# ScalarE scales the first nine token tiles, with two joint reciprocals; VectorE builds a second state table earlier

## The chip, the cores and the metric

The kernel runs on one core of a Trainium2 chip. The metric is the device time of one execution, in microseconds (us). The engines are TensorE (PE in the profile), VectorE (DVE), ScalarE (ACT), GpSimd (POOL) and SyncE (SP, which here only issues DMAs). Each engine works through its own instruction stream in order; streams wait for one another through semaphores.

## The reference, cut to what matters

One layer of a hybrid diffusion backbone in float32, for 1024 latent tokens and 128 context tokens of width 1024:

```python
def _layer(x, cvec, p, rows, h0):
    sh1, sc1, g1, sh2, sc2, g2 = _adaln(cvec, p["w_ada"], p["b_ada"])   # silu(c) @ w_ada + b_ada, six parts
    h = _rmsnorm(x, p["norm_mix"]) * (1 + sc1) + sh1                    # x * rsqrt(mean(x*x) + eps) * g
    proj = jnp.dot(h, p["w_in"])
    pool_out = _pool_mixer(proj[..., :D_POOL], p["pool_w"], p["pool_scale"], rows)
    ssm_out, finals = _ssm_mixer(proj[..., D_POOL:], p, h0)             # diagonal state space, both directions
    mix = jnp.dot(jnp.concatenate([pool_out, ssm_out], axis=-1), p["w_out"])
    x = x + g1 * mix
    h = _rmsnorm(x, p["norm_mlp"]) * (1 + sc2) + sh2
    f = jnp.square(jax.nn.relu(jnp.dot(h, p["w_mlp1"])))
    return x + g2 * jnp.dot(f, p["w_mlp2"]), finals
```

The change touches the first `_rmsnorm`, the division of each token by its root mean square, and the point in time at which one of the weight tables for `_ssm_mixer` (powers of the diagonal times the input matrix) is computed.

## The kernel before, in words

The tokens are nine tiles of 128 tokens by 1024 channels, `XS[0]` to `XS[8]`, the last one the context. The order of all work is written out by hand: one block of code for each engine, with semaphores between them. The opening, up to the input projection, goes as follows.

- **TensorE** forms two parts of the conditioning rows, shift and scale: 16 weight tiles of w_ada (`ada_unit`, L1344, two matmuls with two output rows each and 512 columns), as they land by DMA, and the bias rows (L1361). Then the four half rows that ScalarE copies out of PSUM (`ROW0`, L589) are turned into columns (L1367), one after the other: there is one `ROW0` buffer, so ScalarE copies half row k only when half row k-1 is turned (`ada_cols`), and TensorE turns it when it is copied (`row_ready`). After the fourth, `turn_tile` (L1377) transposes the token tiles one by one; it waits for the scaled tile (`xn`), before tile 1 also for the finished conditioning columns (`ada0`), and from tile 2 on for `affine` to have freed the PSUM banks of the tile two before. Beside tiles 4 to 8 run parts of the first two blocks of the input projection (`project`, L1331 to L1333: three passes with the high and low halves of both operands).
- **ScalarE** computes for each tile, as it lands, the sum of squares (`stats`, L538) and the root (L540, semaphore `root`), then the four half rows, then half of each `affine` (L549), the rounding of the result into its high half (L555) and the high halves of the weights (L576).
- **VectorE** computes the tables of the discretised state matrix, its powers, the table `power_chain` (L1017 to L1028) and one 128x1024 state table, `to_state(1, 1, 0, 0)` (L926, L927, L930). It then scales the nine tiles (`normed`: a reciprocal of one column, L949, and a multiply by it, L950), waits for the four turned half rows (`ada_cols`), makes the conditioning columns out of them (L974, L1041, semaphore `ada0`), and goes on to its half of `affine` (L959) and to the low halves (L964, L969). After the ninth low half seven more state tables follow, with two or three low halves of weights between them; the last of the seven is `to_state(1, 1, 1, 7)`, in front of `split_lo(4)`, and then comes the scan over the states (L1061 to L1069), whose stages wait for ScalarE's copies of the states (`st_act`).
- **TensorE** turns the state tables (`turn_wb`, L1421) between blocks of the input projection, four matrices at a time, as VectorE's tables (`wbt`, for the first one `wbt_first`) come.

Of the later stages only their order matters here: input projection and first scan, kernels of the state space and second scan, output projection, a second normalisation (where ScalarE already scales the tiles by a column, L826), and from about 420 us on the MLP.

Of the kernel before, what the change touches and what calls it, by code (L numbers as in the profile page):

```python
# [19 lines left out]
ALU = mybir.AluOpType  # L20
ACT = mybir.ActivationFunctionType
# [6 lines left out]
TT = T // P  # L28
TG = 384
NG = T // TG  # L30
L = 8
# [31 lines left out]
def build(nc, x_prompt, x_sample, state_ssm, c, c_ctx, norm_mix, norm_mlp, w_ada, b_ada, w_in, w_out, pool_w,  # L63
          pool_scale, ssm_a_re, ssm_a_im, ssm_log_dt, ssm_b_re, ssm_b_im, ssm_c_re, ssm_c_im, ssm_d,
          ssm_w_glu, w_mlp1, w_mlp2, norm_out, inv_count, y_prompt, y_sample, new_state):
    V, S, PE, GP = nc.vector, nc.scalar, nc.tensor, nc.gpsimd
# [57 lines left out]
    STAT = [STATS[:, i, :] for i in range(3)]  # L124
# [60 lines left out]
    def scratch(name, shape):  # L185
# [10 lines left out]
             "wbt", "wbt_first", "wbt_mm", "wb_ready", "st_mm", "st_part", "st_act", "st_dve", "cs_in", "c_mm", "c_ready", "dd_in", "dd_ready",  # L196
             "pad_zero", "rz_zero", "pad_act", "pad_read", "inv_in", "inv_read", "pooled", "pw_in", "map_mm", "map_ev",
             "ca_ready", "kk_mm", "kk_ready", "loc_in0", "loc_in1", "filled", "cx_h", "y_mm", "y_ev", "yd_w0", "yd_w1", "yd_g", "yr0", "yr1", "yr2",
             "row2", "cols2", "gates_w", "acts", "part_ev", "gated", "xt_in0", "xt_in1", "xc_in", "root_inv", "gb_in", "y_split_hi", "y_split", "so", "so_hi",
             "mix_hi", "mix_pool", "mix_ready", "acc", "f_ready", "fin_mm", "fin_ready", "fin_out", "no_in",  # L200
             "y_final", "out_w", "tabs", "ada0", "sqr"]
    sem = {n: nc.alloc_semaphore(n) for n in names}
    s = type("Sems", (), sem)
# [311 lines left out]
    def _(act):  # L515
# [21 lines left out]
        def stats(t, src, dump, base):  # L537
            S.activation(dump, src, ACT.Square, accum_out=STAT[0][:, t:t + 1]).then_inc(s.sq, 1)  # L538
            act.wait_ge(s.sq, base + t + 1)
            S.activation(STAT[1][:, t:t + 1], STAT[0][:, t:t + 1], ACT.Sqrt, bias=EPSB[:], scale=1.0 / D).then_inc(s.root, 1)  # L540
# [35 lines left out]
            S.activation(w_split_bufs(w)[0][:], RAW[n % 4][:], ACT.Copy).then_inc(s.w_hi, 1)  # L576

        act.wait_ge(s.tabs, 2)
        for t in range(TT):
            act.wait_ge(x_in[t], 16 if t < L else 16 * L)  # L580
            stats(t, XS[t][:], SQ0[:], 0)

        n_row = 0
        for part in range(2):
# [68 lines left out]
        for a in range(NG * N_IN):  # L653
            i, g = IN_SEQ[a]
            project(a)
            for k in WB_AT.get(a, ()):
                turned_wb(k)
            if g == NG - 1 and i + 2 < N_IN:
                split_hi(i + 2, FIRST_IN + i + 2)
            if a in (7, 8):  # L660
                for p_ in range(8 * (a - 7), 8 * (a - 6)):
                    if p_ == 12:
                        act.wait_ge(s.wbt, 7)
                    states_out(p_)
            for b in C_AT.get(a, ()):
                c_out(b)
# [200 lines left out]
    def _(dve):  # L867
        count = [0]

        def then(ins):  # L870

            count[0] += 1
            ins.then_inc(s.dve, 1)
            dve.wait_ge(s.dve, count[0])
# [43 lines left out]
        def to_state(b, d, h, ready):  # L918
            gs = slice(b * GB + 8 * h, b * GB + 8 * h + 8)
            q0 = d * G + gs.start  # L920
            out = WB[b][:, d, 8 * h:8 * h + 8, :].rearrange("n g (j p) -> n g j p", p=SP)
            powers = [t_[:, L - 1::-1, q0:q0 + 8] if d == 0 else t_[:, 0:L, q0:q0 + 8] for t_ in (PR, PI)]
            pr, pi = (t_.rearrange("n e q -> n q e").unsqueeze(3).to_broadcast([P, 8, L, SP]) for t_ in powers)
            b1, b2 = (t_[:, q0:q0 + 8, :].unsqueeze(2).to_broadcast([P, 8, L, SP]) for t_ in (B1, BY))
            tmp = TPQ[:, 0:8 * P].rearrange("n (g j p) -> n g j p", g=8, p=SP)
            tt(tmp, b2, pi, ALU.mult).then_inc(s.dve, 1)  # L926
            tt(out, b1, pr, ALU.mult).then_inc(s.dve, 1)  # L927
            count[0] += 2
            dve.wait_ge(s.dve, count[0])
            tt(out, out, tmp, ALU.add).then_inc(s.wbt if ready else s.wbt_first, 1)  # L930
            dve.wait_ge(s.wbt if ready else s.wbt_first, max(ready, 1))

        def from_state(b, d, h):
            q0 = d * G + b * GB + 8 * h
# [8 lines left out]
            dve.wait_ge(s.dve, count[0])  # L943
            tt(out, out, tmp, ALU.add).then_inc(s.ca_ready, 1)
            dve.wait_ge(s.ca_ready, 4 * b + 2 * d + h + 1)

        def normed(t, src, dst, base):
            dve.wait_ge(s.root, base + t + 1)
            then(V.reciprocal(STAT[2][:, t:t + 1], STAT[1][:, t:t + 1]))  # L949
            ts(dst, src, STAT[2][:, t:t + 1], None, ALU.mult).then_inc(s.xn, 1)  # L950

        def affine(t, ht, ada, base):
            cond = 0 if t < L else 1
# [62 lines left out]
        def power_chain():  # L1016
# [3 lines left out]
            for i in range(6):  # L1020
# [7 lines left out]
                then(ts(di, di, 2.0, None, ALU.mult))  # L1028
                sr, si = AR_[i][:], AI_[i][:]

        power_chain()
        to_state(1, 1, 0, 0)
        for t in range(TT):
            normed(t, XS[t][:], XS[t][:], 0)
        dve.wait_ge(s.ada_cols, 4)
        for k in range(4):
            cols = BANK[7][:, 64 + 8 * k:72 + 8 * k].rearrange("p (k a) -> p a k", a=2)
# [152 lines left out]
        to_state(1, 0, 0, 5)  # L1190
        split_lo(3, FIRST_IN + 3)
        to_state(1, 0, 1, 6)
        to_state(1, 1, 1, 7)
        split_lo(4, FIRST_IN + 4)
        def beside_first(k):
            if k in SPLIT_AT:
# [128 lines left out]
    def _(pe):  # L1325
# [80 lines left out]

        def turn_wb(k):
            b, d, i = k // 8, k // 4 % 2, k % 4
            if k in (12, 13):
                pe.wait_ge(s.wbt_first, 1)  # L1410
            else:
                pe.wait_ge(s.wbt, min(k // 2 + 1, 7))
            if k == 0:
                pe.wait_ge(s.aff_a, 4 * TT)
                pe.wait_ge(s.aff_d, 4 * TT)
            if 4 <= k < 8 or k >= 12:
                pe.wait_ge(s.wb_ready, k - 3)
            elif k >= 8:
                pe.wait_ge(s.st_act, k + 5)
            for q in range(4):  # L1420
                last = PE.transpose(BANK[4 + k % 4][:, q * P:(q + 1) * P], WB[b][:, d, 4 * i + q, :], ID[:])  # L1421
            last.then_inc(s.wbt_mm, 1)
# [278 lines left out]
```

## Time and profile before

| | us |
|---|---|
| median of 3 runs (lowest, highest) | 1302.23 (1300.67, 1304.34) |
| the profiled execution | 1306.17 |
| its span, first to last instruction | 1304.1 |

| engine | busy us | share of the span |
|---|---|---|
| TensorE, matmul | 1219.2 | 93% |
| VectorE | 857.9 | 66% |
| GpSimd | 473.4 | 36% |
| ScalarE | 329.1 | 25% |

The mean granted clock of TensorE is 0.968 of full speed. The busy share is an average over stages: TensorE is busy nearly throughout from about 82 us on, with gaps up to 315 us, and mostly waits before that. What a change in the opening is worth has to be read from the engines' instructions in order of time, and from what each of them waited for.

### The profile page before, as it was taken

The page shows a single profiled execution, that of the slowest core. Times are in us where ns is not written, and L with a number is a line of the kernel's source. Part 1 is how long each engine was busy: PE and PEld are TensorE (multiplying, and loading weights), DVE is VectorE, ACT ScalarE, POOL GpSimd, SP SyncE. Part 2 cuts the span into 40 slices and gives each one's busy share as a digit, 9 for nine tenths or more (in the row PEclk, how much of TensorE's full clock was granted, in tenths as well). Part 3 has the DMA queues.
Part 4 walks back from the last instruction along what each step waited for, and adds up shares of the span by engine and source line. Part 5 has one row for each costly group of instructions (what it writes and reads, how often), then busy time and mean ns, then how long its engine had stood idle before and what let it go on. Part 6 is the DMA issues. An engine that isn't in the chain of part 4 may idle for free.

```text
span 1304.1 us, 18626 instructions
## 1 busy us (share of the span) xinstructions
PE 1219.2 (93%) x6479; PEld 1057.5 (81%) x6479; DVE 857.9 (66%) x1343; ACT 329.1 (25%) x613; POOL 473.4 (36%) x394
## 2 busy tenths in 40 slices
PE   3779989895899999999999999999999999999994
PEld 0179978564697888899899899899899899899893
DVE  2988798999886487564564564664664664654658
ACT  2374333222523476011011011011011011021023
POOL 1100000220100341743733733734724724625626
PEclk9979999887899999999999999999999999999997
DMA  8913423875611332120120120110110110210004
GB/s 182 320 34 105 111 74 102 242 175 144 203 42 61 91 104 81 33 65 25 39 64 16 48 64 16 48 58 22 48 49 18 62 48 16 64 48 16 32 0 145
DMA packets 79369, 101.63 MB, mean 78 GB/s; under 512 B 25762, under 2 KB 61766, under 8 KB 79076
## 3 DMA queue, kind: packets, MB, share of 16 engines
q1 hardware_dynamic: 56848, 80.00, 20.2%
q0 software_dynamic: 5200, 17.67, 4.6%
q10 hardware_dynamic: 17284, 3.47, 1.4%
q8 instruction: 23, 0.38, 0.1%
q14 instruction: 14, 0.11, 0.0%
HBM read 89.53 MB, written 9.49 MB: 76 GB/s over the span
## 4 chain that ended last, share of the span: by engine, by line
PE 80%; DVE 8%; issue 3%; DMA 3%; POOL 2%; ACT 2%; ACTq 1%; SPq 0%; POOLq 0%; DVEq 0%
PE bank L1331 23%; PE bank L1332 23%; PE bank L1333 23%; DMA raw<-in_w_ada 2%; POOL acc L511 2%; PE bank L1344 2%; PE bank L1524 1%; PE bank L1523 1%; PE bank L1463 1%; ACTq L525 1%; PE bank L1377 1%; PE bank L1522 1%; DVE x_lo L964 1%; DVE fold_p L1063 1%; DVE fold_q L1061 1%
## 5 line engine op out<-in xcount | busy, mean ns | idle before, releaser
L511 POOL TENSOR_TENSOR acc<-acc,gated 128x512 f32<-128x512 f32 x288 | 401.4, 1394 | 400.7 <-DVE gated L1295 361.6
L1331 PE MATMUL bank<-x_hi,w_hi 128*128 128x384 f32 x960 | 325.2, 339 | 4.2 <-issue 2.7
L1332 PE MATMUL bank<-x_lo,w_hi 128*128 128x384 f32 x960 | 322.4, 336 | 0.0
L1333 PE MATMUL bank<-x_hi,w_lo 128*128 128x384 f32 x960 | 322.3, 336 | 0.0
L1295 DVE TENSOR_TENSOR gated<-bank,gate_b 128x512 f32<-128x512 f32 x288 | 194.1, 687 | 115.9 <-PE bank L1333 87.5
L1331 PE MATMUL bank<-w_hi,f_hi 128*128 128x512 f32 x576 | 224.4, 390 | 1.8 <-DVE w_lo L1276 1.2
L1333 PE MATMUL bank<-w_hi,f_lo 128*128 128x512 f32 x576 | 224.4, 390 | 0.0
L1332 PE MATMUL bank<-w_lo,f_hi 128*128 128x512 f32 x576 | 224.4, 390 | 0.0
L850 ACT ACTIVATE relu<-bank 128x384 f32<-128x384 f32 x96 | 47.2, 492 | 649.5 <-PE bank L1333 646.5
L1285 DVE TENSOR_TENSOR f_tmp<-relu 128x384 f32<-128x384 f32 x96 | 66.4, 691 | 211.6 <-ACT relu L850 211.6
L1331 PEld LDWEIGHTS bank<-x_hi,w_hi 128*128 128x128 f32 x960 | 181.4, 189 | 8.3 <-issue 6.6
L1332 PEld LDWEIGHTS bank<-x_lo,w_hi 128*128 128x128 f32 x960 | 181.5, 189 | 0.6
L1333 PEld LDWEIGHTS bank<-x_hi,w_lo 128*128 128x128 f32 x960 | 181.4, 189 | 0.0
L1331 PEld LDWEIGHTS bank<-w_hi,f_hi 128*128 128x128 f32 x576 | 108.1, 188 | 25.0 <-DVE w_lo L1276 1.5
L1333 PEld LDWEIGHTS bank<-w_hi,f_lo 128*128 128x128 f32 x576 | 108.1, 188 | 22.6
L1332 PEld LDWEIGHTS bank<-w_lo,f_hi 128*128 128x128 f32 x576 | 108.1, 188 | 22.1
L1276 DVE TENSOR_TENSOR w_lo<-raw,w_hi 128x1024 fp32r<-128x1024 f32 x62 | 96.4, 1554 | 0.0
L841 ACT ACTIVATE w_hi<-raw 128x1024 fp32r<-128x1024 f32 x62 | 63.7, 1053 | 0.0
L1289 DVE TENSOR_TENSOR f_lo<-f_tmp,f_hi 128x384 fp32r<-128x384 f32 x96 | 53.6, 558 | 3.3
L1344 PE MATMUL bank<-raw,vector_cols 128*2 128x512 f32 x64 | 31.2, 632 | 22.0 <-ACT vector_cols L527 16.4
L499 POOL TENSOR_TENSOR acc<-acc,x_again 128x512 f32<-128x512 f32 x18 | 25.0, 1391 | 54.0 <-DVE acc L1181 54.0
L1344 PEld LDWEIGHTS bank<-raw,vector_cols 128*2 128x2 f32 x64 | 4.9, 88 | 46.6 <-issue 17.6
(301 smaller groups left out, 1422.1 us busy)
## 6 DMA issues: line engine op xcount, KB each, us to landing
raw<-in_w_mlp SPq DMA_DIRECT2D x64, 512.0 KB
raw<-in_w_ada SPq DMA_DIRECT2D x48, 512.0 KB
x_tile<-in_x_sample POOLq DMA_DIRECT2D x8, 512.0 KB, 8.5
raw<-in_w_in SPq DMA_DIRECT2D x8, 512.0 KB
raw<-in_w_out SPq DMA_DIRECT2D x8, 512.0 KB
x_again<-in_x_sample POOLq DMA_DIRECT2D x8, 512.0 KB, 3.8
out<-acc SPq DMA_DIRECT2D x8, 512.0 KB, 2.6
u_rows<-proj ACTq DMA_DIRECT2D x4, 576.0 KB, 3.1
```

What stands on the lines that cost most here:

```text
L499: GP.tensor_tensor(ACC[:, t, half], ACC[:, t, half], XT[t % 2][:, half], ALU.add).then_inc(s.acc, 1)
L511: GP.tensor_tensor(a, a, BT[i % 4][:], ALU.add).then_inc(s.acc, 1)
L841: S.activation(w_split_bufs(w)[0][:], RAW[n % 4][:], ACT.Copy).then_inc(s.w_hi, 1)
L850: S.activation(RL[i % 2][:], BANK[i % 4][:, 0:TG], ACT.Relu).then_inc(s.ev_act, 1)
L1276: tt(lo[:], RAW[n % 4][:], hi[:].bitcast(F32), ALU.subtract).then_inc(s.w_split, 1)
L1285: tt(FT[i % 2][:], RL[i % 2][:], RL[i % 2][:], ALU.mult).then_inc(s.sqr, 1)
L1289: tt(FL[:, m, cols], FT[i % 2][:], FH[:, m, cols].bitcast(F32), ALU.subtract).then_inc(s.f_ready, 1)
L1295: tt(BT[i % 4][:], BANK[(6 + i) % 4][:], GBT[:, cond, (i % 2) * 512:(i % 2) * 512 + 512], ALU.mult).then_inc(s.ev_dve, 1)
L1331: mm(out, sh_, mh, start=first, stop=False)
L1332: mm(out, sh_, ml, start=False, stop=False)
L1333: return mm(out, sl, mh, start=False, stop=last)
L1344: last = mm(BANK[banks[hf]][0:2, :], cv, RAW[n % 4][:, hf * 512:hf * 512 + 512], start=(k == 0), stop=False)
```

## The change

ScalarE scales the nine tiles by itself, after all nine roots and in front of the half rows, with the instruction `Copy` and a column as its scale. VectorE makes the reciprocals in two instructions, one for the first seven tiles ahead of `power_chain` and one for the last two behind it. The state table `to_state(1, 1, 1)` moves from behind `to_state(1, 0, 1)` to directly behind `to_state(1, 1, 0)`, ahead of the wait for `ada_cols`, and counts on another semaphore (`wbt_first`), so that the waits for `wbt` are counted anew.

```diff
         act.wait_ge(s.tabs, 2)
+        def normed(t):
+            act.wait_ge(s.root_inv0, 1 if t < L - 1 else 2)
+            S.activation(XS[t][:], XS[t][:], ACT.Copy, scale=STAT[2][:, t:t + 1]).then_inc(s.xn, 1)
+
         for t in range(TT):
             act.wait_ge(x_in[t], 16 if t < L else 16 * L)
             stats(t, XS[t][:], SQ0[:], 0)
+        for t in range(TT):
+            normed(t)
...
                     if p_ == 12:
-                        act.wait_ge(s.wbt, 7)
+                        act.wait_ge(s.wbt, 6)
...
-            tt(out, out, tmp, ALU.add).then_inc(s.wbt if ready else s.wbt_first, 1)
-            dve.wait_ge(s.wbt if ready else s.wbt_first, max(ready, 1))
+            tt(out, out, tmp, ALU.add).then_inc(s.wbt if ready > 0 else s.wbt_first, 1)
+            dve.wait_ge(s.wbt if ready > 0 else s.wbt_first, ready if ready > 0 else 1 - ready)
...
-        def normed(t, src, dst, base):
-            dve.wait_ge(s.root, base + t + 1)
-            then(V.reciprocal(STAT[2][:, t:t + 1], STAT[1][:, t:t + 1]))
-            ts(dst, src, STAT[2][:, t:t + 1], None, ALU.mult).then_inc(s.xn, 1)
...
+        dve.wait_ge(s.root, L - 1)
+        V.reciprocal(STAT[2][:, 0:L - 1], STAT[1][:, 0:L - 1]).then_inc(s.root_inv0, 1)
         power_chain()
+        dve.wait_ge(s.root, TT)
+        V.reciprocal(STAT[2][:, L - 1:TT], STAT[1][:, L - 1:TT]).then_inc(s.root_inv0, 1)
         to_state(1, 1, 0, 0)
-        for t in range(TT):
-            normed(t, XS[t][:], XS[t][:], 0)
+        to_state(1, 1, 1, -1)
         dve.wait_ge(s.ada_cols, 4)
...
         to_state(1, 0, 1, 6)
-        to_state(1, 1, 1, 7)
         split_lo(4, FIRST_IN + 4)
...
-            if k in (12, 13):
-                pe.wait_ge(s.wbt_first, 1)
+            if k >= 12:
+                pe.wait_ge(s.wbt_first, k // 2 - 5)
             else:
-                pe.wait_ge(s.wbt, min(k // 2 + 1, 7))
+                pe.wait_ge(s.wbt, k // 2 + 1)
```

## Rows read from the trace of the kernel before

**Rows 1.** Windows: busy us of each engine in a stretch, and the granted clock

```profile
core 0: us, PE busy (x) PEld busy (x) DVE busy (x) ACT busy (x) POOL busy (x), PEclk, DMA share, GB/s
...
62.00:66.30 4.30, 2.09 (x18) 1.77 (x18) 4.12 (x11) 1.76 (x3) 0.00 (x0) 0.70 0.48 143
66.30:74.50 8.20, 7.00 (x32) 6.03 (x32) 6.16 (x20) 4.72 (x10) 0.00 (x0) 0.54 0.00 1
...
82.00:87.00 5.00, 4.81 (x18) 4.75 (x19) 2.49 (x6) 0.65 (x1) 0.00 (x0) 0.50 0.15 45
```

**Rows 2.** Chain of waits, 0 to 330 us: start, duration, what

```profile
62.55 0.59 ACT ada_row L589
...
65.65 0.58 PE bank L1367 x4
66.24 1.90 PE bank L1377 x8
68.14 1.17 issue
69.31 1.95 PE bank L1377 x8
```

**Rows 3.** ScalarE in order of time: start, duration, line, out<-in [idle before]

```profile
54.84 0.57 ACT L589 ACTIVATE ada_row<-bank 2x512 f32<-2x512 f32 x1
...
65.01 0.59 ACT L589 ACTIVATE ada_row<-bank 2x512 f32<-2x512 f32 x1 [0.73 <-PE bank L1367]
69.24 1.50 ACT L549 ACTIVATE h_tile<-bank,ada_cols,ada_cols 128x128 f32<-128x128 f32 x4 [3.64 <-DVE ada_cols L1041]
71.29 1.50 ACT L549 ACTIVATE h_tile<-bank,ada_cols,ada_cols 128x128 f32<-128x128 f32 x4 [0.54 <-PE bank L1377]
```

**Rows 4.** VectorE in order of time, 56 to 70 us

```profile
56.79 1.22 DVE L926 TENSOR_TENSOR fold_pq<-b_im_re,pow_im 128x1024 f32<-128x1024 f32 x1
...
60.44 0.16 DVE L949 RECIPROCAL stats<-stats 128x1 f32<-128x1 f32 x1
...
68.19 0.74 DVE L974 SCALAR_TENSOR_TENSOR ada_cols<-bank,vector_cols 128x4 f32<-128x4 f32 x4
```

**Rows 5.** The nine scaling instructions by tile: shortest, median, longest ns, first and last start

```profile
L950 DVE TENSOR_SCALAR x_tile<-x_tile,stats x9: 752/753/754, 60.6 to 67.5; 128x1024 f32<-128x1024 f32 x9
```

**Rows 6.** ScalarE in order of time, in the second normalisation

```profile
470.75 1.16 ACT L826 ACTIVATE xn_tile<-acc,stats 128x1024 f32<-128x1024 f32 x1 [1.81 <-DVE stats L1263]
471.81 1.04 ACT L555 ACTIVATE x_hi<-h_tile 128x1024 fp32r<-128x1024 f32 x1
```

**Rows 7.** TensorE in order of time, 62 to 195 us

```profile
62.05 0.41 PE L1367 MATMUL bank<-identity,ada_row 2*128 2x2 f32 x4
...
82.19 0.66 PE L1331 MATMUL bank<-x_hi,w_hi 128*128 128x384 f32 x1 [2.74 <-issue]
...
83.28 0.52 PE L1331 MATMUL bank<-x_hi,w_hi 128*128 128x384 f32 x1
83.60 0.52 PE L1332 MATMUL bank<-x_lo,w_hi 128*128 128x384 f32 x1
...
97.38 0.33 PE L1332 MATMUL bank<-x_lo,w_hi 128*128 128x384 f32 x1
97.55 0.33 PE L1333 MATMUL bank<-x_hi,w_lo 128*128 128x384 f32 x1
...
194.74 1.03 PE L1463 MATMUL bank<-raw,vector_cols 128*2 128x256 f32 x8 [3.55 <-DMA raw<-in_w_ada]
```

**Rows 8.** VectorE in order of time, 70 to 218 us

```profile
73.77 1.22 DVE L964 TENSOR_TENSOR x_lo<-h_tile,x_hi 128x1024 fp32r<-128x1024 f32 x1 [1.11 <-ACT x_hi L555]
...
129.02 1.23 DVE L930 TENSOR_TENSOR to_state_b<-to_state_b,fold_pq 128x1024 f32<-128x1024 f32 x1
135.65 1.23 DVE L969 TENSOR_TENSOR w_lo<-raw,w_hi 128x1024 fp32r<-128x1024 f32 x1 [5.40 <-ACT w_hi L576]
...
217.51 1.23 DVE L940 TENSOR_TENSOR fold_pq<-c_turned,pow_im 128x1024 f32<-128x1024 f32 x1 [3.02 <-PE bank L1333]
```

More of the change, by code:

```diff
@@ L198, in build @@
              "ca_ready", "kk_mm", "kk_ready", "loc_in0", "loc_in1", "filled", "cx_h", "y_mm", "y_ev", "yd_w0", "yd_w1", "yd_g", "yr0", "yr1", "yr2",
-             "row2", "cols2", "gates_w", "acts", "part_ev", "gated", "xt_in0", "xt_in1", "xc_in", "root_inv", "gb_in", "y_split_hi", "y_split", "so", "so_hi",
+             "row2", "cols2", "gates_w", "acts", "part_ev", "gated", "xt_in0", "xt_in1", "xc_in", "root_inv", "root_inv0", "gb_in", "y_split_hi", "y_split", "so", "so_hi",
              "mix_hi", "mix_pool", "mix_ready", "acc", "f_ready", "fin_mm", "fin_ready", "fin_out", "no_in",
```

## The prediction, made before the changed kernel was run

> **What bounds the kernel now.** I read the windows first: from 82 us on TensorE is busy almost throughout, while between 62 and 82 us it waits for ScalarE and VectorE and runs at the lower level of its clock for most of the time (granted 0.70, then 0.54, then 0.50, where 0.50 is 1.2 GHz) [rows 1]. The change edits this opening and moves one table, so the question is what sets the moment at which TensorE's unbroken work starts, 82.19 us [rows 7], and whether anything later depends on what VectorE has saved.
>
> The chain of waits answers the first part [rows 2]. It goes through ScalarE's copies of the half rows and TensorE's turning of them, four times back and forth, then through tile 0, then through a pause of 1.17 us that the trace calls "issue", then tile 1. The pause ends at 69.31; ScalarE's first affine starts at 69.24, released by VectorE's conditioning columns [rows 3]. The code has the same condition in front of tile 1 (`ada0`), so the pause is VectorE's: it ends its scaling at 68.19 and only then makes the columns, although the fourth half row has been turned at about 66.2 [rows 4, 2]. So two arms run to tile 1: the half rows (ready at 66.24) and VectorE (ready at 69.24). VectorE's is the late one. After tile 1 the chain is rounding and subtracting: affine of tile 1 at 71.29, first low half at 73.77, and so on without a gap on VectorE until the low half of tile 2, which opens the projection at 82.19 [rows 3, 8, 7]. A shift of tile 1 is a shift of the projection.
>
> **The change, part by part.**
>
> *VectorE loses the nine scalings.* They fill 60.44 to 68.19, 7.75 us: nine multiplies of 0.753 us, each behind a reciprocal of 0.16 us [rows 4, 5]. Two reciprocals come instead. No row shows one of 128x7 or 128x2; from below each is worth the 0.16 us of 128x1, from above hardly more than the 1.22 us of a 128x1024 multiply [rows 4]. I take 0.2 us each, nearest to the first. The waits in front of them cost nothing that is seen: the second is reached at about 57.0 us, and all nine roots are done by 54.84, when ScalarE has gone on to the half row [rows 3, 4].
>
> *VectorE gains one state table ahead of `ada_cols`.* The table there now runs from 56.79 to 60.44, 3.65 us for three instructions [rows 4]. With the reciprocals both tables run from about 57.2 to 64.5 us. Then VectorE waits for the fourth turned half row, where it now arrives late. This arm gets 3.7 us earlier, and is no longer the one that ends last if the half rows stay where they are or move back.
>
> *ScalarE gains nine scalings, and all four half rows are queued behind them.* This is the term that decides. In program order they stand between the last root and the first half row. The same instruction runs in the second normalisation: 1.16 us, and the next instruction on ScalarE starts 1.06 us after it [rows 6]. Nine follow one another: 9 x 1.06 = 9.5 us. ScalarE starts them at 54.84, where now the first half row starts, and is done at 64.4. From below, if they cost no more than copies without a column (1.04 us long, of which some 0.1 overlaps, [rows 6]), it is 8.5 us; from above, with no overlap, 10.4. I take 9.5. Beside it on VectorE run the tables; no row shows that two engines slow each other here. The first reciprocal is there by about 49 us, before ScalarE asks; the second is there at 57.2, tile 7's turn comes at 62.
>
> *The half rows.* Before, the first had been copied at 54.84 and lay waiting when TensorE finished its conditioning matmuls, so that the first turn ran at 62.05 [rows 3, 7]. Now the first copy starts at 64.4. One full step of the ping-pong is 0.73 + 0.59 = 1.32 us [rows 3]; at the faster clock level a turn takes 0.41 instead of 0.58 us [rows 7, 2], but TensorE has rested by then and I count all at 1.32. Three steps on, the fourth copy starts at 64.4 + 3.96 = 68.3. From the fourth copy's start to tile 0 it was 66.24 - 65.01 = 1.23 us [rows 2, 3], so tile 0 starts at 69.6 instead of 66.24: 3.3 us later.
>
> *Tile 1.* VectorE makes the columns while tile 0 is turned (about 1.05 us after the turn, against 1.90 us for tile 0), so the pause of 1.17 us is gone [rows 2, 4]. Tile 1 is late by 3.3 - 1.17 = 2.2 us, and affine 1, ScalarE's and VectorE's rounding and the projection with it: 84.4 instead of 82.19.
>
> *The table that left.* `to_state(1, 1, 1, 7)` ends at 130.25 (the last instruction starts at 129.02 and takes 1.23), and behind it VectorE sits idle for 5.40 us until ScalarE's high half of the weights lets it go on at 135.65 [rows 8]. In the code that high half waits for the ninth block of the projection, because it overwrites the weights that the block reads. The 3.65 us saved there lengthen a pause from 5.4 to 9.0 us, and nothing starts earlier. The scan behind it moves with TensorE. Were the cover gone, up to 3.65 us could be gained there; this is the lower bound of this part, and zero the upper one.
>
> *After that* everything is counted from TensorE's work: the scan releases the weight buffer for which TensorE waits 3.55 us before 194.74, and VectorE waits 3.02 us for TensorE before 217.51 [rows 7, 8]. Both ends of both waits move by the same amount. No transfer there is issued at a time of its own.
>
> *The clock.* After 82 us TensorE runs for some 5 us at the lower level: matmuls of the projection follow one another every 0.32 us there and every 0.17 us at 97 us [rows 1, 7]. Each us at the lower level costs about 0.46 us. A start that is 2.2 us later may make this stretch shorter or longer. If all of the 5 us went, the gain would be 2.3 us, and as long again would cost 2.3 us; I take zero.
>
> The sum, against the profiled execution (1306.17 us, span 1304.1): +3.3 for the half rows, -1.17 for the pause, 0 for the moved table, 0 for the clock: +2.2, that is 1308.4. The profiled execution lies 3.9 us above the median of the runs shown, so on that scale 1302.23 + 2.2 = 1304.4 us. This is 0.17%, below the 0.3% (3.9 us) that a measurement of this kernel can tell from no change.
>
> One rule of the Trainium skill speaks to the scalings. In "ScalarE: Activation LUTs", section "What ACT_TABLE_LOAD costs", a change of the activation table set costs about 2.66 us, and the section on table sets adds that cheap functions such as copy are in every set. By the first alone the root followed by the copy would add 2.66 us to the sum, by the second nothing; the trace agrees with the second, since L826 runs between roots without a load ahead of it [rows 6].
>
> **The rivals.**
>
> 1. *VectorE's lead comes through.* If ScalarE's block did not delay the half rows (because TensorE's conditioning matmuls, bound by DMA, end later than 62 us in most executions), tile 0 would stay and the pause would go: -1.17. If the scan also started early, -3.65 more: 1302.23 - 4.8 = 1297.4 us, faster. For it: the pause is real, and VectorE is the late arm now. Against it: the half rows are behind 9.5 us of ScalarE's work by program order, and the 5.40 us of idle time in front of the scan show that VectorE is not what the scan waits for. The point from which tile 1 comes earlier than before: tile 0 late by less than 1.17 us, so scalings of less than (9.5 - 2.2) / 9 = 0.81 us each, or matmuls that end over 2.2 us later.
>
> 2. *The low clock lasts longer* (the slower side). TensorE now rests before the half rows and again before the projection. For it: at 66 to 74 us it was busy for 7.0 of 8.2 us and was granted 0.54 only [rows 1]. Each us longer at the low level costs 0.46 us; beyond the 2.2 us, 1.7 us more makes it over 0.3%, which takes 3.7 us more of low clock. If it lasted over the whole of the projection's first part, up to 97 us, some 9 us at the high level would take 17 instead: +8, or 1312 us. Against it: once the projection runs TensorE has no gap, before as after. The Trainium skill ("TensorE: Matmul & The Clock Gate", Part 1) says that the count of slow matmuls differs from run to run with the same kernel, which would spread the result and not move it.
>
> 3. *No net shift.* The two shifts of the opening cancel: scalings at 8.5 us, two of the turns at the faster level (-0.3), and a shorter low clock after 84 us (-1): 2.2 - 1.0 - 0.3 - 1 = about 0, or 1302.2 us. For it: the bounds allow it. Against it: it needs all three.
>
> 4. *The change does not do what it says*: the first scaling waits for a reciprocal that comes only behind the power chain. By the code it stands ahead of it. If it did come behind, at 57.2 us, the scalings would start 2.4 us later and the time would be 1306.8 us.
>
> **How the numbers follow.** The forecast (half rows late, +1 to +3.5) has 0.68; rival 3 has 0.12, rival 1 has 0.06, rival 2 has 0.09, rival 4 has 0.02, and 0.03 is left for what I don't see. The range: from below 2.2 - 1.0 (cheap scalings) - 2.3 (no slow stretch) is -1.1, or 1301.1; from above 2.2 + 0.9 (no overlap) + 2.3 is +5.4, or 1307.6, of which I leave out the last 0.4, since both ends at once are unlikely: 1301.1 to 1307.2 us. Slower by over 0.3% is rival 2 for the most part, half of rival 4 and the upper end of the forecast: 0.12. Faster by over 0.3% is rival 1 and little else: 0.05. Within 0.3%: 0.83.
>
> **What would show it.** In the changed kernel's trace: ScalarE's nine scalings from about 54.9 to 64.4 us, 1.05 to 1.06 us apart, with no table load; TensorE's first turn of a half row at 65, not 62; tile 0 near 69.6 and tile 1 right behind it; VectorE idle from 64.5 to 69.5; the projection at 84.4; VectorE's idle time before `split_lo(4)` near 9 us, and the scan about 2.2 us later than 136.9. The prediction is wrong if the projection starts before 82.2 us, if the scan starts earlier than before, or if the difference that stands at 84 us has changed by more than 2 us at 217 us for a reason other than the clock.

## The result, and the profile after

The changed kernel takes 1306.1 us (median of 20 runs, 1303.27 to 1309.87); the kernel before took 1302.88 us in the same series (20 runs, 1300.67 to 1306.01). The ratio is 1.0025 with a 95% interval of 1.0017 to 1.0033: slower by 2.2 to 4.3 us, within the 0.3% named ahead for the point value, with an upper end a little above it. A second series of the same change gave 1.0018 (1.0009 to 1.0027); one of its twelve runs took 3055 us, is marked slow and is left out of that ratio (its median, 1306.17, has it in). The forecast was 1304.4 us, +2.2 us, in a range of 1301.1 to 1307.2.

The profiled execution of the changed kernel took 1306.23 us (span 1304.2), almost exactly that of before (1306.17, span 1304.1). But 1306.23 is close to the median of its kernel, and 1306.17 lies above all twenty runs of the kernel before: the profile of before is one of its slowest executions (mean granted clock 0.968, against 0.973 in the profile after). The loss is in the opening all the same. ScalarE in order of time (start, duration, line, out<-in, idle time before and what ended it), the counterpart of [rows 3]:

```profile
53.72 1.06 ACT L538 ACTIVATE square_dump<-x_tile 128x1024 f32<-128x1024 f32 x1 [3.11 <-DMA x_tile<-in_x_prompt]
...
55.10 9.45 ACT L581 ACTIVATE x_tile<-x_tile,stats 128x1024 f32<-128x1024 f32 x9
64.45 0.57 ACT L595 ACTIVATE ada_row<-bank 2x512 f32<-2x512 f32 x1
...
68.74 0.59 ACT L595 ACTIVATE ada_row<-bank 2x512 f32<-2x512 f32 x1 [1.08 <-PE bank L1370]
71.98 2.91 ACT L549 ACTIVATE h_tile<-bank,ada_cols,ada_cols 128x128 f32<-128x128 f32 x8 [2.66 <-PE bank L1380]
```

The nine scalings fill 55.10 to 64.55 us with no table load (this trace has its loads, 1.28 us each, at 26.40 and then at 271.69 us), and the first half row is copied at 64.45; before, it was copied at 54.84. TensorE, the counterpart of [rows 7]:

```profile
60.29 1.87 PE L1364 MATMUL bank<-ada_bias,constants 1*2 1x512 f32 x4
65.08 0.58 PE L1370 MATMUL bank<-identity,ada_row 2*128 2x2 f32 x4 [2.91 <-ACT ada_row L595]
...
69.38 0.58 PE L1370 MATMUL bank<-identity,ada_row 2*128 2x2 f32 x4 [1.08 <-ACT ada_row L595]
69.89 3.34 PE L1380 MATMUL bank<-identity,x_tile 128*128 128x128 f32 x16
...
84.28 0.66 PE L1334 MATMUL bank<-x_hi,w_hi 128*128 128x384 f32 x1 [2.73 <-issue]
```

TensorE waits 2.91 us for the first half row, and tile 0 starts at 69.89 instead of 66.17. Tiles 0 and 1 now follow one another (x16 in one row); the pause of 1.17 us of [rows 2] is gone. The projection starts at 84.28 instead of 82.19, 2.09 us later. VectorE, the counterpart of [rows 4 and 8]:

```profile
62.15 1.23 DVE L936 TENSOR_TENSOR to_state_b<-to_state_b,fold_pq 128x1024 f32<-128x1024 f32 x1
70.07 0.75 DVE L975 SCALAR_TENSOR_TENSOR ada_cols<-bank,vector_cols 128x4 f32<-128x4 f32 x4 [6.69 <-PE bank L1370]
...
137.81 1.22 DVE L970 TENSOR_TENSOR w_lo<-raw,w_hi 128x1024 fp32r<-128x1024 f32 x1 [9.07 <-ACT w_hi L576]
...
219.66 1.23 DVE L946 TENSOR_TENSOR fold_pq<-c_turned,pow_im 128x1024 f32<-128x1024 f32 x1 [3.00 <-PE bank L1336]
```

VectorE has both tables done at 63.4 (62.15 + 1.23) and then waits 6.69 us for the half rows. In front of `split_lo(4)` it waits 9.07 us instead of 5.40: the 3.65 us of the moved table went into that pause, and the next work starts 2.16 us later than before (137.81 against 135.65). At the start of the third table group it is 2.15 us (219.66 against 217.51).

Behind 220 us this pair of profiles loses the difference again. About 1 us of it is a single instruction of VectorE, which took 1.22 us in the profile of before and 0.18 in that of after. VectorE and GpSimd in order of time, first in the kernel before, then in the changed one:

```profile
282.43 1.22 DVE L1108 COPY states_b<-first_states 128x16 f32<-128x16 f32 x1
282.43 1.18 POOL L460 MEMSET padded<- 128x1296 f32 x1 [5.10 <-DMA local_b<-kernels_b]
```

```profile
280.41 1.18 POOL L460 MEMSET padded<- 128x1296 f32 x1 [5.00 <-DMA local_b<-kernels_b]
284.70 0.18 DVE L1112 COPY states_b<-first_states 128x16 f32<-128x16 f32 x1
```

In the profile of before the copy starts together with a MEMSET of GpSimd and ends with it, to 0.04 us. In the other twelve traces of this document the two don't overlap, and the copy takes 0.18 us. That the one delays the other is suggested by this, not shown.

The rest is the clock in the gated output (GLU). These are windows of TensorE (busy us and count, granted clock, DMA), first before, then after:

```profile
348.30:352.00 3.70, 3.69 (x12) 0.50 0.96 321
352.00:356.00 4.00, 4.00 (x20) 0.77 0.96 359
```

```profile
349.60:352.00 2.40, 2.35 (x7) 0.50 1.01 265
352.00:356.00 4.00, 4.00 (x23) 0.92 0.97 373
```

TensorE starts this stage 1.34 us later after the change (349.65 against 348.31), but spends 2.5 us less at the lower level (3.70 + 0.46 x 4.00 = 5.5 us against 2.40 + 0.16 x 4.00 = 3.0; a window granted 0.77 of full speed is at half speed for 46% of it), which is 1.25 us of work. The MLP's first relu is at 508.43 against 508.23. So a pair of profiles whose spans agree within 0.1 us holds a loss of 2.15 us and two events in stages that the edit does not touch. The time of one profiled execution would have said "no change"; the stage by stage comparison and the medians say +2 to +3. A second pair of traces, at the end of the experiments, shows how far such stage times move by themselves.

### The profile page after: what moved, and what is told of

Its sections match the earlier page's. It is cut to its first block, busy times and chain, and to the rows that moved or that the text cites. A ratio compares the mean times of both kernels' runs of the same rounds, so it can differ in the third digit from the quotient of the medians.

```text
span 1304.2 us, 18621 instructions
## 1 busy us (share of the span) xinstructions
PE 1213.0 (93%) x6479; PEld 1054.3 (81%) x6479; DVE 846.6 (65%) x1327; ACT 338.6 (26%) x622; POOL 474.7 (36%) x394
## 4 chain that ended last, share of the span: by engine, by line
PE 79%; DVE 8%; issue 3%; DMA 3%; ACT 3%; POOL 2%; ACTq 1%; SPq 0%; POOLq 0%; DVEq 0%
PE bank L1334 23%; PE bank L1335 23%; PE bank L1336 23%; POOL acc L511 2%; DMA raw<-in_w_ada 2%; PE bank L1527 1%; PE bank L1526 1%; PE bank L1466 1%; ACTq L525 1%; PE bank L1347 1%; PE bank L1525 1%; DVE x_lo L965 1%; DMA x_tile<-in_x_prompt 1%; DVE fold_p L1067 1%; ACT x_tile L581 1%
## 5 line engine op out<-in xcount | busy, mean ns | idle before, releaser
L1335 PEld LDWEIGHTS bank<-w_lo,f_hi 128*128 128x128 f32 x576 | 108.1, 188 | 22.1
```

Of the source, the lines that this page charges most:

```text
L1335: mm(out, sh_, ml, start=False, stop=False)
```

## The experiments

Each ran beside the kernel before on the same chip. "Projection" is the start of the first projection matmul in its trace; 82.19 us before, 84.28 after the change. The edits are cut to the lines that matter; the counts of the waits for `wbt` and `wbt_first` go with the place of the table.

| kernel | ratio to before (95% interval) | median us | projection us |
|---|---|---|---|
| the change | 1.0025 (1.0017 to 1.0033) | 1306.1 | 84.28 |
| the change, again | 1.0018 (1.0009 to 1.0027) | 1306.17 | 84.46 |
| scalings only | 1.0019 (1.0010 to 1.0029) | 1306.04 | 82.76 |
| table only | 1.0026 (1.0014 to 1.0037) | 1306.9 | 84.94 |
| first half row ahead | 1.0003 (0.9993 to 1.0014) | 1303.11 | 83.92 |
| four more copies | 1.0047 (1.0032 to 1.0061) | 1309.48 | 88.80 |
| scalings in ScalarE's waits | 0.9993 (0.9984 to 1.0002) | 1303.21 | 81.42 |
| scalings shared | 0.9986 (0.9975 to 0.9997) | 1302.09 | 81.56 |
| waits filled, early weight halves | 0.9964 (0.9951 to 0.9978) | 1298.9 | 77.41 |
| the same, again | 0.9976 (0.9964 to 0.9988) | 1300.21 | 77.58 |
| and early half rows | 0.9962 (0.9947 to 0.9977) | 1298.24 | 77.63 |
| the kernel before, again | 1.0003 (0.9991 to 1.0015) | 1303.41 | 82.79 |

The kernel before had medians of 1302.97, 1304.38 and 1303.66 us in the three groups of runs (rows 3 to 6, then row 2 with rows 7 to 9, then the last three), so the ratios are what can be compared across groups.

TensorE's mean granted clock in each run is on record too, and it explains much of the scatter. Over the 189 runs of the three groups (all but the one of 3055 us) it lies between 0.966 and 0.978, and between runs of one kernel the time falls by about 0.5 us for each 0.001 (least squares over these runs: 0.52, 0.45 to 0.59). Set to one clock by this estimate, the change costs 2.35 us (1.6 to 3.1) in its second series and "scalings only" 2.15 (1.4 to 2.9). The edit may itself move the mean clock, so this is an estimate and not a measurement; the runs of the kernel before in the first series have no clock on record.

**Scalings only.** The moved table goes back to its place:

```diff
-        to_state(1, 1, 1, -1)
         dve.wait_ge(s.ada_cols, 4)
...
         to_state(1, 0, 1, 6)
+        to_state(1, 1, 1, 7)
```

> Only the first part of the change: ScalarE scales the nine tiles with joint reciprocals, while the second state table stays where it was, behind to_state(1, 0, 1). Queue theory (the half rows are late because they are queued behind nine scalings on ScalarE, and VectorE has nothing to do with it): the same as the whole change, projection at 84.3 us in the trace, +2.2 us or more on the median (1305 to 1306), VectorE's idle time before split_lo(4) back at 5.4 us. Rival (the moved table costs the 1 us by which the measured +3.2 us exceeds the 2.2 us of the trace): the projection also at 84.3, but a median 1 us lower than that of the whole change.

The ratio, 1.0019, is that of the whole change. The projection stands at 82.76 and not at 84.3, which looks like a miss until the row of the scalings is read:

```profile
51.96 1.06 ACT L538 ACTIVATE square_dump<-x_tile 128x1024 f32<-128x1024 f32 x1 [3.02 <-DMA x_tile<-in_x_prompt]
...
53.34 9.45 ACT L581 ACTIVATE x_tile<-x_tile,stats 128x1024 f32<-128x1024 f32 x9
```

In this execution the last token tile landed 1.8 us earlier, and the scalings started at 53.34 instead of 55.10. From there to the projection it is 29.4 us, against 29.2 with the whole change. VectorE's idle time in front of `split_lo(4)` is back at 5.41 us: the table's time comes out of the pause and goes back into it. The rival's 1 us doesn't show in the medians (1306.04 against 1306.1), but with intervals of about 1.2 us to either side they don't exclude it either; that the moved table is worth nothing rests on the pause, in this trace and in the next one.

**Table only.** VectorE keeps the scalings, with the second table ahead of them:

```diff
         to_state(1, 1, 0, 0)
+        to_state(1, 1, 1, -1)
         for t in range(TT):
             normed(t, XS[t][:], XS[t][:], 0)
...
-        to_state(1, 1, 1, 7)
```

> Only the second part of the change: VectorE builds the second state table ahead of its nine scalings, which it keeps. Queue theory: VectorE was the late arm, so its 3.65 us appear in full: scalings end at 68.19 + 3.65 = 71.8, columns at 72.9, tile 1 right after, projection at 82.19 + 3.65 = 85.8 us, median +3.7 us (1306.5), and the 3.65 us saved in front of split_lo(4) give nothing back (idle time there 9 us). Rival (VectorE's lead reaches the scan): the shift is 3.65 us at the projection and is 0 at the start of the scan, median unchanged.

```profile
55.88 1.23 DVE L926 TENSOR_TENSOR fold_pq<-b_im_re,pow_im 128x1024 f32<-128x1024 f32 x1
...
70.94 0.75 DVE L974 SCALAR_TENSOR_TENSOR ada_cols<-bank,vector_cols 128x4 f32<-128x4 f32 x4
...
138.43 1.23 DVE L969 TENSOR_TENSOR w_lo<-raw,w_hi 128x1024 fp32r<-128x1024 f32 x1 [9.06 <-ACT w_hi L576]
```

The columns start at 70.94, 2.75 us late and not 3.65, because VectorE reached its first table at 55.88 in this execution and at 56.79 in [rows 4]: 3.65 - 0.91 = 2.74. The projection is 2.75 us late, and `split_lo(4)` 2.78 us. A lead of 3.65 us in front of the scan gave nothing back, which settles the rival of the lead. The edit alone costs about what the whole change costs (+0.26%, expected +3.7 us or 0.28%): moved without the scalings, the table lengthens the arm that ends last.

**First half row ahead of the scalings.**

```diff
+        act.wait_ge(s.ada_mm, 1)
+        S.activation(ROW0[:], BANK[0][0:2, :], ACT.Copy).then_inc(s.row_ready, 1)
         for t in range(TT):
             normed(t)
```

> The whole change, with the copy of the first half row put ahead of the nine scalings on ScalarE. Queue theory: the first turn runs at about 62 us again, the second copy starts when the scalings end, at 65.1 us instead of 65.75, so tile 1 and the projection come 0.65 us earlier than with the whole change (83.6 us), +1.5 us against the kernel before. Rival (TensorE's low clock during the turns is what costs): two turns at the faster level give only 0.3 us.

```profile
65.18 0.57 ACT L600 ACTIVATE ada_row<-bank 2x512 f32<-2x512 f32 x1
```

```profile
83.92 0.66 PE L1339 MATMUL bank<-x_hi,w_hi 128*128 128x384 f32 x1 [3.41 <-issue]
```

The second copy starts at 65.18, the projection at 83.92. The scalings start at 55.83, behind the copy (0.48 us), and the last root was 0.25 us later than after the change, so the expected 0.65 us shrinks to 0.4 in the trace and is 0.6 with that taken out. The median says -2.2 us against the change (ratio 1.0003 against 1.0025). The interval ends at 1.0014, just below that of the change's first series (from 1.0017) and inside that of its second (1.0009 to 1.0027), so whether there is more in it than the 0.6 us of the trace stays open. Part of it is likely the clock: these runs have 0.9740 on average and those of the change 0.9726, which by the estimate above is 0.7 us.

**Four more copies** between the scalings and the half rows:

```diff
+        act.wait_ge(s.xn, TT)
+        for t in range(4):
+            act.wait_ge(s.more, t)
+            S.activation(SQ0[:], XS[8][:], ACT.Copy, scale=STAT[2][:, 0:1]).then_inc(s.more, 1)
```

> The whole change and four more copies of 128x1024 with a column as scale on ScalarE, between the nine scalings and the first half row; their output is not used. Queue theory: every us on ScalarE there is a us of the whole time: 4 x 1.06 = 4.2 us and some 0.3 us for waits between them, projection at 88.8 us, median +4.5 us against the whole change (1310.6), with VectorE idle for 4.5 us more in front of the columns. Rival (something else sets the half rows, as the clock or the end of the conditioning matmuls): less than 2 us more.

```profile
55.02 9.45 ACT L581 ACTIVATE x_tile<-x_tile,stats 128x1024 f32<-128x1024 f32 x9
64.50 4.69 ACT L591 ACTIVATE square_dump<-x_tile,stats 128x1024 f32<-128x1024 f32 x4
69.10 0.57 ACT L599 ACTIVATE ada_row<-bank 2x512 f32<-2x512 f32 x1
```

The half row is 4.65 us later than after the change, and the projection 4.52 us (88.80, as expected); against the second trace of the change (half row at 64.39, projection at 84.46) it is 4.71 and 4.34. The whole time rises by 6.1 us against the kernel before (ratio 1.0047, 1.0032 to 1.0061), 2.9 us more than the change did; the 4.5 expected lie inside what the two intervals allow, and so would the rival's 2 us: it is the trace that rules the rival out. What ScalarE does in this place is paid nearly one for one at the projection.

**Scalings in ScalarE's waits.** Between the sums ScalarE waits for tiles to land. Five scalings go there, four stay behind the first half row; the reciprocals are made for five tiles and for four:

```diff
         for t in range(TT):
             act.wait_ge(x_in[t], 16 if t < L else 16 * L)
             stats(t, XS[t][:], SQ0[:], 0)
+            for u in {5: (0,), 6: (1,), 7: (2, 3, 4)}.get(t, ()):
+                normed(u)
+        act.wait_ge(s.ada_mm, 1)
+        S.activation(ROW0[:], BANK[0][0:2, :], ACT.Copy).then_inc(s.row_ready, 1)
-        for t in range(TT):
+        for t in range(5, TT):
             normed(t)
```

> The whole change, with five of ScalarE's nine scalings moved into its waits for the tiles (one behind tile 5's sum, one behind tile 6's, three behind tile 7's; one reciprocal of five columns stands among VectorE's b_bar operations, one of four behind the power chain), then the first half row, then the other four scalings. Queue theory: ScalarE is free again at about 60 us, before the matmuls end at 62.1, so the second half row is on time; tile 0 at 66.2 to 66.5, and since VectorE is idle from 63.4 the pause in front of tile 1 is gone too: tile 1 1.2 us earlier than in the kernel before, 3.4 us earlier than with the whole change, projection at 80.9 us, median 1301.8. Rival (scalings on ScalarE cost about 1 us each wherever they stand): no better than the whole change, 1305 to 1306.

```profile
62.31 0.41 PE L1377 MATMUL bank<-identity,ada_row 2*128 2x2 f32 x4
63.46 0.43 PE L1377 MATMUL bank<-identity,ada_row 2*128 2x2 f32 x4 [0.74 <-ACT ada_row L602]
...
66.81 4.81 PE L1387 MATMUL bank<-identity,x_tile 128*128 128x128 f32 x24
```

**Scalings shared.** VectorE keeps tiles 0 to 4, ScalarE takes 5 to 8; the table stays at its old place:

```diff
+        for t in range(5, TT):                       # ScalarE
+            act.wait_ge(s.root_inv0, 1 if t < L - 1 else 2)
+            S.activation(XS[t][:], XS[t][:], ACT.Copy, scale=STAT[2][:, t:t + 1]).then_inc(s.xn, 1)
...
+        for t in range(5):                           # VectorE
+            ts(XS[t][:], XS[t][:], STAT[2][:, t:t + 1], None, ALU.mult).then_inc(s.xn, 1)
...
-            pe.wait_ge(s.xn, base + t + 1)
+            pe.wait_ge(s.xn, max(base + t + 1, TT))
```

> The kernel before, with the scalings shared: VectorE scales tiles 0 to 4 behind its first state table, ScalarE tiles 5 to 8 behind the last root, with the joint reciprocals; the second state table stays at its old place. TensorE waits for all nine in front of tile 0. Queue theory: ScalarE is done at 55.1 + 4.2 = 59.3, before the matmuls end, VectorE at 60.2 + 5 x 0.67 = 63.6 instead of 68.19; both arms are on time, tile 0 at 66.2, no pause, tile 1 1.2 us earlier than before, projection at 80.9 us, median 1301.8, the same as with the scalings in ScalarE's waits. Rival (any scaling on ScalarE delays): slower than before by about 1 us.

The fence is of the first of the two. Both put the turns back behind the bias rows (62.31 and 62.70 us, with no idle time between), tile 0 at 66.81 and 66.95, and the projection at 81.42 and 81.56. The bias rows ended 0.3 and 0.6 us later than in [rows 7]'s execution, which is half and all of what the projection lacks to 80.9; in the first of the two the last step of the ping-pong also has 1.08 us of ScalarE's idle time instead of 0.73. Against the change the ratio falls from 1.0018 in the same group to 0.9993 and 0.9986, 3 to 4 us. Against the kernel before the first can't be told from no change (interval up to 1.0002), the second is just below it. The scalings on ScalarE cost nothing that these runs show where ScalarE has time, and the joint reciprocals and the second engine are no loss in themselves; the place in the queue was. The rival that scalings cost about 1 us each wherever they stand falls.

**Waits filled, and the first two weight blocks split early.** On top of the first of these two, the high halves of weight blocks 0 and 1 go behind the scalings and behind the last half row on ScalarE, the low halves behind the second table and behind the columns on VectorE, instead of between the roundings of the first tiles:

```diff
         for t in range(5, TT):
             normed(t)
+        split_hi(0, FIRST_IN)
...
+        split_hi(1, FIRST_IN + 1)                    # ScalarE, behind the last half row
         act.wait_ge(s.ada0, 2)
...
         to_state(1, 1, 1, -1)
+        split_lo(0, FIRST_IN)
         dve.wait_ge(s.ada_cols, 4)
...
         dve.wait_ge(s.ada0, 2)
+        split_lo(1, FIRST_IN + 1)
         affine(0, HT0, 0, 0)
...
             round_lo(t, HT0, 0)
-            if t < 2:
-                split_lo(t, FIRST_IN + t)
```

> As the one with five scalings in ScalarE's waits, and the first two weight blocks are split into their high and low halves ahead of the tiles' affine (high halves on ScalarE behind the scalings and behind the last half row, low halves on VectorE behind the second state table and behind the columns), where both engines are idle, instead of between the first tiles' roundings. Queue theory: the stretch from tile 1's affine to the third low half is work of VectorE without a gap; two low halves of 1.14 us leave it, so the projection starts 2.3 us earlier again, at about 78.7 us, and the median is 3.4 us below the kernel before (1299.5). Rival (the weight blocks land by DMA only after 62 us, or TensorE's turning of tiles 2 to 4 bounds this stretch): 1 us or less.

VectorE's part of the opening in it:

```profile
61.12 1.23 DVE L943 TENSOR_TENSOR to_state_b<-to_state_b,fold_pq 128x1024 f32<-128x1024 f32 x1
62.38 1.22 DVE L977 TENSOR_TENSOR w_lo<-raw,w_hi 128x1024 fp32r<-128x1024 f32 x1
65.40 0.75 DVE L982 SCALAR_TENSOR_TENSOR ada_cols<-bank,vector_cols 128x4 f32<-128x4 f32 x4 [1.79 <-PE bank L1377]
66.18 0.24 DVE L1053 COPY ada_cols<-bank 128x8 f32<-128x8 f32 x2
66.45 1.23 DVE L977 TENSOR_TENSOR w_lo<-raw,w_hi 128x1024 fp32r<-128x1024 f32 x1
```

The projection starts at 77.41, 4.8 us earlier than before; the bias rows ended 1.1 us earlier in this execution, so 3.7 us are left for the three edits together. The distance between the two is 16.35 us instead of 20.07, and 2.7 us less than without the early halves (81.42 - 62.38 = 19.04), where 2.3 were expected. The first low half stands in the time in which VectorE waited for the half rows. The ratio is 0.9964 (0.9951 to 0.9978), from only five runs, so it ran again:

> The kernel with filled waits and early weight halves once more, beside the others: 5 us below the kernel before on the median (0.996), as in the first run; the projection starts 16.3 to 16.4 us after the bias rows' end (77.41 - 61.06), 3.8 us less than in the kernel before (82.19 - 62.12 = 20.1). Rival (the first run's gain was partly a run in which the tiles landed early): ratio 0.998.

77.58 us and 0.9976 (0.9964 to 0.9988): faster than the kernel before in both series, by about 3 to 5 us. The 0.996 expected lies just outside the interval and the rival's 0.998 inside; but the intervals of the two series overlap, so whether the first one flattered it can't be told. The gain stays either way. Its runs also have a higher mean clock than those of the kernel before (0.9756 and 0.9755 against 0.9721 and 0.9734), and whether the edit brings that is open; set to one clock by the estimate above, 2.7 us (2.1 to 3.3) are left. The distance from the bias rows' end is 16.60 us.

**Early half rows** on top of that. The two half rows of the first part are copied and turned between the weight tiles of the second:

```diff
+            if t in (5, 6):                          # ScalarE, among the sums
+                act.wait_ge(s.ada_mm, 1)
+                if t == 6:
+                    act.wait_ge(s.ada_cols, 1)
+                S.activation(ROW0[:], BANK[t - 5][0:2, :], ACT.Copy).then_inc(s.row_ready, 1)
...
+                if part == 1 and k in (1, 3):        # TensorE, among the weight tiles
+                    row_turn(k // 2)
```

> As the one with filled waits and early weight halves, and the two half rows of the first part (complete at 42.8 us) are copied and turned while TensorE still waits for the second part's weight tiles, so that two of the four steps of the ping-pong are left behind the last matmul. Queue theory: from the end of the bias rows to tile 0 it is 2.5 us instead of 4.1 to 4.2, the projection starts about 1.7 us earlier relative to that end, and the median is 1.7 us below that of the kernel without it (1297.2). Rival (by now VectorE's two tables and the weight halves bound the columns): 0.5 us or less.

```profile
65.51 3.44 PE L1396 MATMUL bank<-identity,x_tile 128*128 128x128 f32 x16
69.93 1.06 PE L1396 MATMUL bank<-identity,x_tile 128*128 128x128 f32 x8 [0.99 <-DVE h_tile L970]
```

From the end of the bias rows to tile 0 it is 2.33 us, as expected (2.5), but the projection starts 14.45 us after that end, so 1.9 to 2.15 us of distance are gained in the trace, while the bias rows themselves ended at 63.18, some 2 us later. In that execution ScalarE's high half of the first block came only at 62.15 and VectorE went from its low half to the columns without waiting (66.28). The ratio, 0.9962 (0.9947 to 0.9977), can't be told from the 0.9964 and 0.9976 without the edit. One execution doesn't settle whether the edit itself delays the matmuls (it puts two turns between them) or the tiles landed late; that stays open.

**The kernel before and the change, once more.**

> The kernel before once more, for a second trace. VectorE sets tile 1 in it and waits neither for the last tile nor for the bias rows, so the columns are ready at 69.2 us after VectorE's own chain, whatever moment the tiles land; ratio 1.000.

```profile
69.84 1.50 ACT L549 ACTIVATE h_tile<-bank,ada_cols,ada_cols 128x128 f32<-128x128 f32 x4 [2.81 <-DVE ada_cols L1041]
```

The columns were ready at 69.84, not 69.2: VectorE's own chain was 0.6 us later, and the projection (82.79) follows it, although ScalarE was done with the last root 1.5 us later and the bias rows ended 1.2 us later than in the execution of [rows 3 and 7]. VectorE is the bound here, as read. The ratio is 1.0003 (0.9991 to 1.0015).

> The whole change once more, for a second trace and for its time beside the others on the same chip. Queue theory: ScalarE's scalings start when the last tile's root is done, so the projection starts 29.2 us after it (84.28 - 55.10), whatever that moment is in this execution, and the median lies 2 to 4 us above the kernel before. Rival (the half rows hang on the end of the conditioning matmuls): the distance from that end (62.1 us) is the constant one.

The scalings start at 55.04 and the projection 29.42 us later; with "scalings only" the three distances are 29.2, 29.4 and 29.4 us. From the end of the bias rows (62.16, 62.32, 61.14) they are 22.1, 22.1 and 21.6, so the first distance is the steadier one, as the queue theory has it, though three traces are few.

Now there are two pairs of traces, and they can be compared stage by stage (start in us):

| stage | before | after | shift | before, again | after, again | shift |
|---|---|---|---|---|---|---|
| projection | 82.19 | 84.28 | 2.09 | 82.79 | 84.46 | 1.67 |
| `split_lo(4)` | 135.65 | 137.81 | 2.16 | 135.94 | 136.98 | 1.04 |
| third table group | 217.51 | 219.66 | 2.15 | 217.12 | 218.20 | 1.08 |
| GLU | 348.31 | 349.65 | 1.34 | 346.53 | 348.10 | 1.57 |
| first relu of the MLP | 508.23 | 508.43 | 0.20 | 505.47 | 508.26 | 2.79 |
| span | 1304.1 | 1304.2 | 0.1 | 1301.2 | 1304.0 | 2.8 |

The second pair loses 0.6 us of the shift right behind the projection's start: up to 92 us TensorE was at the lower level for about 4.8 us before (granted 0.74 over 9.21 us) and for about 3.5 us after (0.77 over 7.54 us), which is 0.65 us of work. In the GLU it goes the other way, by 1.2 us. So the steady 2.1 us of the first pair from 84 to 217 us are in part luck, and a stage time of one pair is good to about 1 us here.

## Why the prediction was right

**What bounds the opening.** That VectorE, and not the half rows, set tile 1 held: the pause that the trace calls "issue" vanished, and "table only" moved tile 1 with VectorE's chain. Of the three clock figures read for 62 to 82 us the last (0.50) is of 82 to 87; nothing rests on it.

**ScalarE's queue.** Nine scalings were put at 9.5 us from the first to the start of what follows, and took 9.35 (9.45 to the end of the ninth). They started at 55.10 and not at 54.84, so that the first half row, put at 64.4, came at 64.45: the two misses cancel. Of the two statements of the Trainium skill ("ScalarE: Activation LUTs") that were weighed, the trace agrees with the one that cheap functions are in every table set: no load stands in front of the scalings, between the loads at 26.40 and 271.69 us. This term carried the forecast, and "four more copies" shows its slope at the projection (4.65 us in, 4.52 us out, or 4.71 and 4.34).

**The half rows.** Three steps at 1.32 us were counted; two took 1.30 and 1.33 and one 1.66 us (ScalarE idle for 1.08 us instead of 0.73 ahead of the fourth copy). That third step has 1.08 in some kernels and 0.73 in others, with the same code around it, and the same in both traces of the kernel before and in both of the change; the traces give no cause. Tile 0 was forecast at 69.6 and came at 69.89. It is 3.72 us late and not 3.3, since in order of time it started at 66.17 before; the 66.24 of the forecast is the start in the chain of waits.

**Tile 1 and after.** The low half of tile 0 is 2.10 us late (75.87 against 73.77), the projection 2.09, forecast 2.2: the late third step cost 0.3, and the two tiles without a pause took 3.34 us together, where 1.90 + 1.95 had been counted; the two errors nearly cancel, which is luck. About 0.2 us of the second miss is the clock, which rose during tile 1 (granted 0.63 from 72 to 73 us); in the second trace of the change it rose after 74 us, and from tile 0 to the projection it took 14.62 us instead of 14.39.

**The moved table** was put at nothing, with a pause of 9.0 us in front of `split_lo(4)`; it is 9.07, and "scalings only" costs the same as the whole within the intervals.

**The clock** was put at nothing. Behind the projection's start the low level lasts as long as before in the first pair (the stretch of 84.2 to 89.2 us has 0.50, as 82 to 87 had [rows 1]), and 1.3 us shorter in the second. Further on it differed in both pairs, in opposite directions. Zero lies between the two; each pair is off from it by about 1 us somewhere, and no trace shows that the change does it.

**The size.** The shift at the projection is 2.09 us in one pair of traces and 1.67 in the other, where 2.2 were forecast; on the medians it is +3.2 us, interval 2.2 to 4.3, and +2.3 (1.2 to 3.5) in the second series. The forecast lies at the lower edge of the first interval and inside the second. What may fill the rest is the clock, by the estimate above (2.35 us at one clock), or a dependence that the forecast named for TensorE's matmuls only: the scalings start when the last token tile has landed and its root is done, and that moment moved between 53.3 and 56.3 us over the thirteen traces (53.34 with "scalings only", 56.30 with the kernel before once more), where the kernel before took no notice of it. No trace shows how it falls in unprofiled runs, so this is argued and not shown.

**The rivals.** The lead of VectorE did not come through; the low clock did not last longer behind the projection; the shifts of the opening did not cancel; the reciprocal came at 47.93 us, in time.

## What to carry to other kernels

Moving work off the engine that ends last is worth what the next arm leaves, and that arm has to be read with the moved work put into its queue: here it cost 9.45 us in front of a ping-pong that had been on time. The same work was free in the receiving engine's waits for DMA, or shared so that both arms ended before the third. When two profiled spans agree, compare the start of each stage before calling it no change: an opposite shift of 2 us was hidden in this pair. And take a second pair before trusting a shift of 1 us, with the granted clock of each execution beside it.

## What the runs showed of the hardware

Scalings of 128x1024 by a column start every 1.04 us back to back on ScalarE (9.35 us from the first to the instruction behind the ninth), also in place and beside VectorE's tables; in the second normalisation it was 1.06 [rows 6]. A reciprocal of 128x7 took 0.20 us and one of 128x2 0.17, against 0.16 for one column. A copy of 128x16 on VectorE took 1.22 us in one trace and 0.18 in twelve; in the one it started together with a MEMSET of GpSimd of 1.18 us. Over 189 runs the time was shorter by about 0.5 us for each 0.001 by which TensorE's mean granted clock was higher.
